# Expert weights of a mixture layer: gate and up blocks loaded in pairs, in another order

## The reference, cut to what matters

```python
probs = softmax(h @ router_w)                       # per group
gate, idx = top_k(swapaxes(probs, 1, 2), cap)       # cap = 64 latent, 16 context tokens per expert
xs = h[b_idx, idx]                                  # 80 rows of 1024 per expert
hid = silu(xs @ wg[e]) * (xs @ wu[e])               # wg, wu: 1024 x 2048 per expert
ye = (hid @ wd[e]) * gate                           # wd: 2048 x 1024 per expert
f = zeros_like(h).at[b_idx, idx].add(ye)
x = x + g2 * rms_norm(f, norm_ffn_post)
```

## Time and profile before

| | |
|---|---|
| median of 3 runs | 1744.59 us (1741.53 to 1746.22) |
| profiled execution | 1750.1 us, its span 1748.2 us |
| PE busy | 1561.2 us (89%), 7025 matmuls |
| DVE busy | 1273.4 us (73%) |
| ACT busy | 997.7 us (57%) |
| POOL busy | 199.1 us (11%) |
| weight queue (q1) | 179184 packets, 453.01 MB, 70.7% of 16 engines |
| packets under 8 KB | 172748 of 189173 |
| SP waits for DVE's `w_lo` before a load (L254) | 996.4 us in 380 waits |

### The profile page before, as it was taken

One profiled execution on the slowest core, in us unless ns is written; L12 is line 12 of the kernel. 1 busy time (PEld: TensorE's weight loads), 2 busy tenths in 40 slices (PEclk: granted clock), 3 DMA queues, 4 the chain that ended last, 5 costly groups with the idle time before them and its releaser, 6 DMA issues.

```text
span 1748.2 us, 19460 instructions
## 1 busy us (share of the span) xinstructions
PE 1561.2 (89%) x7025; PEld 1063.8 (61%) x7025; DVE 1273.4 (73%) x1133; ACT 997.7 (57%) x813; POOL 199.1 (11%) x100
## 2 busy tenths in 40 slices
PE   5799988978957999999999999998999999999992
PEld 3588766655854666666666665665665666666561
DVE  5525544774476888888888887887888878888883
ACT  6223345142334676666666676666676666766761
POOL 5411222144000000000000000000000000000000
PEclk8799999888957999999999999999999999999996
DMA  9321112347234899999999999999999999999983
GB/s 345 107 66 55 49 49 75 106 141 275 84 133 163 333 367 347 373 335 354 365 350 369 341 348 360 337 381 322 349 357 338 380 324 371 357 343 377 333 322 127
DMA packets 189173, 476.73 MB, mean 273 GB/s; under 512 B 11470, under 2 KB 13770, under 8 KB 172748
## 3 DMA queue, kind: packets, MB, share of 16 engines
q1 hardware_dynamic: 179184, 453.01, 70.7%
q0 software_dynamic: 3072, 10.49, 2.5%
q10 hardware_dynamic: 6876, 12.68, 2.1%
HBM read 462.51 MB, written 13.64 MB: 272 GB/s over the span
## 4 chain that ended last, share of the span: by engine, by line
PE 31%; DVE 22%; DMA 20%; ACT 13%; issue 12%; POOL 2%; ACTq 0%; SPq 0%; DVEq 0%; POOLq 0%
DVE w_lo L266 12%; ACT w_hi L260 11%; DMA raw<-in_exp_down 7%; DMA raw<-in_exp_gate 6%; DMA raw<-in_exp_up 4%; PE bank L298 4%; PE bank L297 4%; PE bank L299 4%; PE bank L934 3%; PE bank L938 3%; PE bank L935 3%; PE bank L919 2%; PE bank L920 2%; PE bank L924 2%; POOL w_lo L266 1%
## 5 line engine op out<-in xcount | busy, mean ns | idle before, releaser
L266 DVE TENSOR_TENSOR w_lo<-raw,w_hi 128x2048 fp32r<-128x2048 f32 (+1 forms) x424 | 946.9, 2246 | 319.8 <-ACT w_hi L260 319.5
L260 ACT CAST w_hi<-raw 128x2048 fp32r<-128x2048 f32 x424 | 805.6, 1910 | 336.6 <-PE bank L299 63.3
L919 PE MATMUL bank<-w_hi,act_lo 128*80 128x512 f32 x1024 | 407.3, 398 | 17.3 <-DVE act_lo L1358 16.7
L920 PE MATMUL bank<-w_hi,act_hi 128*80 128x512 f32 x1024 | 402.9, 393 | 0.0
L924 PE MATMUL bank<-w_lo,act_hi 128*80 128x512 f32 x1024 | 277.7, 392 | 0.7 <-DVE w_lo L266 0.7
L934 PE MATMUL bank<-w_hi,act_lo 128*80 128x512 f32 x512 | 206.4, 403 | 35.1 <-DVE act_lo L1369 34.9
L919 PEld LDWEIGHTS bank<-w_hi,act_lo 128*80 128x80 f32 x1024 | 154.3, 151 | 99.2 <-issue 16.3
L924 PEld LDWEIGHTS bank<-w_lo,act_hi 128*80 128x80 f32 x1024 | 151.3, 148 | 85.7 <-DVE w_lo L266 2.7
L935 PE MATMUL bank<-w_hi,act_hi 128*80 128x512 f32 x512 | 202.3, 395 | 0.0
L920 PEld LDWEIGHTS bank<-w_hi,act_hi 128*80 128x80 f32 x1024 | 152.2, 149 | 78.2 <-issue 0.5
L1469 POOL DMA_INDIRECT f_rows<-arena,slot_tok x16 | 26.7, 1671 | 1118.6 <-ACT arena L623 1118.6
(11 more groups left out here) (204 smaller groups left out, 1415.7 us busy)
## 6 DMA issues: line engine op xcount, KB each, us to landing
raw<-in_exp_gate SPq DMA_DIRECT2D x128, 1024.0 KB, 5.9
raw<-in_exp_up SPq DMA_DIRECT2D x128, 1024.0 KB, 6.6
raw<-in_exp_down SPq DMA_DIRECT2D x128, 1024.0 KB, 6.2
raw<-in_ada_w SPq DMA_DIRECT2D x24, 1024.0 KB, 5.5
raw<-in_w_in SPq DMA_DIRECT2D x12, 1024.0 KB, 5.0
arena<-in_x_lat ACTq DMA_DIRECT2D x8, 512.0 KB, 9.4
raw<-in_w_out SPq DMA_DIRECT2D x4, 1024.0 KB, 5.4
xn_rows<-arena SPq DMA_DIRECT2D x5, 512.0 KB, 2.6
```

Of the source, the lines that this page charges most:

```text
L260: nc.scalar.copy(w_hi[:, n % WS, :], raw[:, n % RAW, :]).then_inc(hi_done, 1)
L266: ops.tensor_tensor(w_lo[:, n % WS, at], raw[:, n % RAW, at], w_hi[:, n % WS, at], ALU.subtract).then_inc(done, 1)
L919: mm(dst, x[1][:, kk, :], wh[:, k, :], start=(kk == 0), stop=False)
L920: mm(dst, x[0][:, kk, :], wh[:, k, :], start=False, stop=False)
```

## The change

Gate and up blocks are taken in pairs: b now counts pairs of blocks (0 or 1), and a chunk of a pair is 2 k-tiles x 1024 columns, in rows of 4 KB. A pair is four chunks (`part` 0..3), and each chunk adds to two PSUM banks: gate pair in banks 0 and 1, up pair in 2 and 3. Matmuls per chunk, their shapes and the two splits stay as they were, and so do RAW and WS. The order of a body becomes g1 (4 chunks), d0, d1 (2 each), u1 (4), g0' (4), d2, d3 (2 each), u0' (4); the last body is g1 u1 d0 d1 d2 d3. Eight chunks (g0, u0) stand in front of the first body instead of six.

What hangs on the order moves with it: both silus of a pair stand at the gate pair's last chunk, both `hidden` at the up pair's last chunk and there ahead of that step's split. `turn_after` says after which chunk a block of `hid` is turned: blocks 0 and 1 after g1's parts 0 and 2, blocks 2 and 3 after g0's parts 0 and 2 (in the last body after d0 and d1). The token transposes stand after steps i = 4 and 8, `gathered` at 5 and 9. On SP the zeroing of `f_rows` comes before the writes of `xn2_rows`, both behind seven expert loads instead of six. The post-norm gain of the expert layer is loaded by SP behind the last weight load, and its products go to regions of their own.

```diff
     def body_chunks(last):
-        order = [("u", 1, 0), ("d", 0, 0), ("g", 2, 0), ("u", 2, 0), ("d", 1, 0), ("g", 3, 0), ("u", 3, 0), ("d", 2, 0)]
-        if not last:
-            order += [("g", 0, 1)]
-        order += [("d", 3, 0)]
-        if not last:
-            order += [("u", 0, 1), ("g", 1, 1)]
-        return [(kind, b, half, nxt) for kind, b, nxt in order for half in range(2)]
-
-    FIRST_CHUNKS = [(kind, b, half) for kind, b in (("g", 0), ("u", 0), ("g", 1)) for half in range(2)]
+        if last:
+            order = [("g", 1, 0), ("u", 1, 0), ("d", 0, 0), ("d", 1, 0), ("d", 2, 0), ("d", 3, 0)]
+        else:
+            order = [("g", 1, 0), ("d", 0, 0), ("d", 1, 0), ("u", 1, 0), ("g", 0, 1), ("d", 2, 0), ("d", 3, 0), ("u", 0, 1)]
+        return [(kind, b, part, nxt) for kind, b, nxt in order for part in range(2 if kind == "d" else 4)]
+
+    FIRST_CHUNKS = [(kind, 0, part) for kind in "gu" for part in range(4)]
+
+    def turn_after(last, kind, b, part):
+        at = {("g", 1, 0): 0, ("g", 1, 2): 1}
+        at.update({("d", 0, 1): 2, ("d", 1, 1): 3} if last else {("g", 0, 0): 2, ("g", 0, 2): 3})
+        return at.get((kind, b, part))
...
         w = {"g": exp_gate, "u": exp_up}[kind]
-        w = w[bass.ds(e, 1), :, b * 512:(b + 1) * 512].rearrange("o (k p) n -> p (o k) n", p=P)
-        return w[:, 4 * half:4 * half + 4, :]
+        w = w[bass.ds(e, 1), :, b * D:(b + 1) * D].rearrange("o (k p) n -> p (o k) n", p=P)
+        return w[:, 2 * part:2 * part + 2, :]
...
# sync
-        for i, (kind, b, half) in enumerate(FIRST_CHUNKS):
-            load(sync, N_EXP + i, 0, expert_source(0, kind, b, half), 512)
+        for i, (kind, b, part) in enumerate(FIRST_CHUNKS[:-1]):
+            load(sync, N_EXP + i, 0, expert_source(0, kind, b, part), D)
+        sync.wait_ge(fz, 1)
+        for t in range(TILES):
+            sync.dma_start(f_rows[t * P:(t + 1) * P, :], zeros).then_inc(f_zero, 16)
         for t in range(TILES):
             sync.wait_ge(xn2_rd, t + 1)
             sync.dma_start(xn2_rows[t * P:(t + 1) * P, :], xn2[:, t, :]).then_inc(xn2_out, 16)
...
# scalar, body
-                if not last and (kind, b, half) == ("g", 3, 0):
-                    gathered_half(e + 1, 1 - pr2, 0)
-                if not last and (kind, b, half) == ("d", 2, 0):
-                    gathered_half(e + 1, 1 - pr2, 1)
+                if not last and i in (5, 9):
+                    gathered_half(e + 1, 1 - pr2, i // 9)
                 ... split_hi(act, N_BODY + i + WS, e)
-                if half and kind == "g":
-                    silu(N_BODY + i, e, b)
-                    if b:
-                        hidT_hi(e + nxt, b - 1)
...
-                if kind == "d" and b == 2 and half:
-                    hidT_hi(e, 3)
+                if kind == "g" and part == 3:
+                    silu(N_BODY + i, e, 2 * b)
+                    silu(N_BODY + i, e, 2 * b + 1)
+                turn = turn_after(last, kind, b, part)
+                if turn is not None:
+                    hidT_hi(e, turn)
...
# tensor
-            for k in range(4):
-                kk = 4 * half + k
-                mm(dst, x[1][:, kk, :], wh[:, k, :], start=(kk == 0), stop=False)
-                mm(dst, x[0][:, kk, :], wh[:, k, :], start=False, stop=False)
+            for kk, dst, j, at in steps:
+                mm(dst, x[1][:, kk, :], wh[:, j, at], start=(kk == 0), stop=False)
+                mm(dst, x[0][:, kk, :], wh[:, j, at], start=False, stop=False)
...
# tensor, body
+                turn = turn_after(last, kind, b, part)
+                if turn is not None:
+                    if turn:
+                        pe.wait_ge(ht_lo, 4 * e + turn)
+                    hid_T(e, turn)
-                if not last and half and kind == "d" and b == 1:
+                if not last and i == 4:
                     gather(e + 1, 0)
-                if not last and half and kind == "u" and b == 3:
+                if not last and i == 8:
                     pe.wait_ge(xs_f, 2 * e + 3)
                     gather(e + 1, 1)
...
# vector, body
+                if not last and i in (5, 9):
+                    gathered(e + 1, i // 9)
+                    gathered_lo(e + 1, 1 - pr2, i // 9)
+                if kind == "u" and part == 3:
+                    hidden(N_BODY + i, e, e + nxt, 2 * b)
+                    hidden(N_BODY + i, e, e + nxt, 2 * b + 1)
                 if not last or i + WS < len(chunks):
                     split_lo(dve, "dve", N_BODY + i + WS, e)
+                turn = turn_after(last, kind, b, part)
+                if turn is not None:
+                    hidT_lo(e, turn)
```

More of the change, by code:

```diff
@@ L259, in split_hi @@
             act.wait_ge(w_used, e * PER_E + (n - WS + 1))
-        nc.scalar.copy(w_hi[:, n % WS, :], raw[:, n % RAW, :]).then_inc(hi_done, 1)
+        nc.scalar.copy(w_hi[:, n % WS, :], landed(n)).then_inc(hi_done, 1)
     def split_lo(eng, who, n, e=0):
@@ L323, in _ @@
             sync.dma_start(xn2_rows[t * P:(t + 1) * P, :], xn2[:, t, :]).then_inc(xn2_out, 16)
-        sync.wait_ge(fz, 1)
-        for t in range(TILES):
-            sync.dma_start(f_rows[t * P:(t + 1) * P, :], zeros).then_inc(f_zero, 16)
+        kind, b, part = FIRST_CHUNKS[-1]
+        load(sync, N_EXP + len(FIRST_CHUNKS) - 1, 0, expert_source(0, kind, b, part), D)
         def body(e, last):
-            for i, (kind, b, half, nxt) in enumerate(body_chunks(last)):
-                load(sync, N_BODY + i, e, expert_source(e + nxt, kind, b, half), D if kind == "d" else 512)
+            for i, (kind, b, part, nxt) in enumerate(body_chunks(last)):
+                load(sync, N_BODY + i, e, expert_source(e + nxt, kind, b, part), D)
         with sync.Fori(0, LAST) as e:
@@ L954, in _ @@
         pe.wait_ge(xs_l, 2)
-        for i, (kind, b, half) in enumerate(FIRST_CHUNKS):
-            up_or_gate(N_EXP + i, 0, b + (2 if kind == "u" else 0), half, xs[0])
-        hid_T(0, 0)
+        for i, (kind, b, part) in enumerate(FIRST_CHUNKS):
+            up_or_gate(N_EXP + i, 0, 2 if kind == "u" else 0, part, xs[0])
         def body(e, pr2, last):
-            for i, (kind, b, half, nxt) in enumerate(body_chunks(last)):
+            for i, (kind, b, part, nxt) in enumerate(body_chunks(last)):
@@ L971, in body @@
                 else:
-                    if half == 0:
+                    if part == 0:
                         pe.wait_ge(ht_lo, 4 * e + (b + 1))
-                    down(n, e, b, half)
-                if half and kind == "g" and b:
-                    if b > 1:
-                        pe.wait_ge(ht_lo, 4 * e + (b - 1))
-                    hid_T(own, b - 1)
-                if not last and half and kind == "d" and b == 1:
+                    down(n, e, b, part)
+                turn = turn_after(last, kind, b, part)
@@ L981, in body @@
+                if turn is not None:
[3 more added lines that the diff above has]
+                if not last and i == 4:
                     gather(e + 1, 0)
-                if not last and half and kind == "u" and b == 3:
+                if not last and i == 8:
                     pe.wait_ge(xs_f, 2 * e + 3)
                     gather(e + 1, 1)
-                if half and kind == "d" and b == 2:
-                    pe.wait_ge(ht_lo, 4 * e + 3)
-                    hid_T(e, 3)
-                    if last:
-                        pe.wait_ge(gbias2, 16)
-                        pe.wait_ge(sl_ev, 4 * NEXP)
-                        gate_rows(rows, (0, 1, 2, 3))
+                if last and kind == "d" and b == 2 and part == 1:
+                    pe.wait_ge(gbias2, 16)
+                    pe.wait_ge(sl_ev, 4 * NEXP)
+                    pe.wait_ge(hid_rd, 4 * NEXP)
+                    gate_rows(rows, (0, 1, 2, 3))
@@ L1248, in _, with gate_row @@
                 split_lo(dve, "dve", n)
-        def gate_row(first, banks):
+        def gate_row(first, banks, gain, dst):
             dve.wait_ge(post_in, 16 * (first // 4 + 1))
@@ L1256, in gate_row @@
                     dve.wait_ge(gr_ps, first + 2 * g + half + 1)
-                    tt(g_row[:, g, at], psum[banks[2 * g + half]][:, :], post[:, at], ALU.mult).then_inc(gr_ev, 1)
-        gate_row(0, (2, 3, 5, 6))
+                    tt(dst[g][:, at], psum[banks[2 * g + half]][:, :], gain[:, at], ALU.mult).then_inc(gr_ev, 1)
+        gate_row(0, (2, 3, 5, 6), post, [g_row[:, 0, :], g_row[:, 1, :]])
         dve.wait_ge(col_rd, 8)
```

115 lines of the change are left out of this document (52 added, 63 removed).

## The result

The changed kernel takes 1803.98 us (median of 5 runs, 1801.48 to 1813.97) against 1744.59 in the same session (1740.65 to 1748.17): ratio 1.035, interval 1.032 to 1.039. It is 59 us slower where 17 were forecast, and lies outside the range.

What follows compares the result with a forecast made beforehand. PE was taken as the bound, waiting for the in-order lists of DVE and ACT. 15 x (0.2 + 0.7) = 13.5, + 5 clock, - 1 last body = +17.5 us; 1744.6 + 17 = 1761 us, range 1734 to 1778.

Steps and rivals of the forecast that it cites:

- What bounds the kernel: In the experts PE is the bound, and it waits for the in-order lists of DVE and ACT.
- The packets: On the weight queue q1, packets were to fall by 65536, to 113.6 thousand.
- "nothing" for the moved SP and POOL steps: Later `xn2_rows` writes and gathers needed earlier were to cost nothing, having enough cover.
- Place A: Behind the gathers, to block 2's turn: PE waits 3.0 us, 2.8 before; +0.2 us per expert.
- The old waits at d2, g0' and d3 are gone: Behind the gathers: these PE waits vanish, as their data has two chunks more of time.
- Place B: Behind the scatter at time s: PE waits 1.9 us at block 1's turn, 1.17 before; +0.7 us per expert.
- The -1 for the last body: The last body loses waits at d0, d1 and d3, some 2 us, and gets one at the turn: -1 us.
- The walk to the turn of block 1: Behind the scatter at s: chunk 3's copy at s + 12.8 plus 4.8 us; PE, there at s + 15.7, waits 1.9.
- the 17 old waits that the prediction counted at d0: Behind the scatter before the change: 17 of 49 PE waits for `hidT_lo`, 1.17 us per expert with tails.
- The clock: PE's clock falls behind waits of about 2 us in 5 of 15 experts instead of 2: +5 us.
- rival 2: Much slower: the clock falls in most experts, at block 2's or block 1's turn; +33 us, 1777; chance 0.13.
- The sum: Whole kernel: 13.5 us of waiting, + 5 for the clock, - 1 for the last body, +17.5 us.

Runs made afterwards that it cites:

- E3: The changed kernel without the indirect gathers (from the second expert on) and scatters (but the last): 1746.6 us, ratio 1.003.
- E4: The kernel before the change without the indirect gathers (from the second expert on) and scatters (but the last): 1729.4 us, ratio 0.993.
- E2: The changed kernel's order, with gate and up chunks of 4 k-tiles x 512 columns in 2 KB rows: 1770.8 us, ratio 1.017.
- E13: The changed kernel with each gate and up chunk loaded by two DMAs of 512 columns, in 2 KB rows: 1804.5 us, ratio 1.035.
- E5: The changed kernel with six landed chunks instead of four in the experts: 1724.4 us, ratio 0.990.
- E6: The changed kernel's order with chunks in 2 KB rows and six landed chunks instead of four: 1724.2 us, ratio 0.989.
- E9: The changed kernel with four unused 512-column matmuls ahead of each wait at the turns of blocks 1 and 2: 1784.4 us, ratio 1.025.
- E11: The changed kernel without the scatters (but the last), gathers kept: 1751.9 us, ratio 1.004.
- E14: The changed kernel with each gate and up chunk loaded by two DMAs of one k-tile, in 4 KB rows: 1801.8 us, ratio 1.035.
- E10: The changed kernel with gate chunks of 4 k-tiles x 512 columns in 2 KB rows, up chunks in 4 KB rows: 1792.5 us, ratio 1.026.
- E15: The changed kernel with up chunks of 4 k-tiles x 512 columns in 2 KB rows, gate chunks in 4 KB rows: 1815.8 us, ratio 1.043.
- E8: The kernel before the change with six landed chunks instead of four: 1714.3 us, ratio 0.984.

## Why the prediction was wrong, step by step

**What bounds the kernel** was read rightly: PE and the in-order lists around it. The packets, the unchanged work of DVE and ACT, and "nothing" for the moved SP and POOL steps held. POOL's first gather, for one, still waits for its slot numbers and not for the later `xn2_rows`, as in the earlier trace rows:

```profile
POOL arena L1460 <- DVE slot_tok L1346: 85.0, 1, 85.0
```

**Place A** was right in size. The forecast had DVE done 25.6 us behind the transpose, 3 us of waiting, 2 of it at the turn; the trace has 25.3 and 1.65. E3 against E4 shows the waiting itself is worth nothing net (+0.2 per expert was said). Its place was right too; its consequence was not, see the clock. "The old waits at d2, g0' and d3 are gone" held.

**Place B is the first step that failed**: "Its load is still issued behind the split of chunk 23, at the same time, behind the same scatter and gather. What differs is the row length", and from that chunk 3 at s + 12.8. The issue came when it said, at s + 3.5 in both kernels, but the load took 10.6 us to land, for 9.5 before (means of 14). Chunk 3 was copied at s + 14.2, and chunk 2, of which nothing was said for the new order, at s + 10.9 instead of 8.8. E2 prices this at 33 of the 59 us. The reasoning went wrong twice. It bounded the new loads' landing by the medians of the earlier trace rows, -0.2 to +0.5 us, but those are over all loads, and what counts is the landing beside a scatter, where the trace of before had no chunk of this shape. And it took row length as the one difference; E13, with the short rows, is as slow, so row length alone is not the cause. The bound should have been as wide as the delay in hand: the scatter already held chunk 3 up by 2.7 us (13.1 for 10.4), so twice that was no remote case, and a chunk 2 that is 2 us late makes the turn of block 0 wait as well, a term that the sum did not have. The -1 for the last body lacked it too: PE waited 3.9 us there. Depth decides whether all this matters (E5 equals E6).

The walk to the turn of block 1 had the right path and a wrong start. From chunk 3's copy at s + 14.2, its 4.8 us give s + 19.0, where s + 17.6 was said. PE came to the turn at about s + 16.1, for 15.7: it ended chunk 23 near s + 6.2 and not 7.0 (s + 5.4 in the expert shown), but lost more than that at block 0. So the wait there is 2.4 us in the mean, and 0.6 at block 0, where 1.9 was said for all of place B. Of the 17 old waits that the prediction counted at d0, 9 are there (9.9 us) and 8 at d1 (3.7 us); their sum is right.

**The clock is the second**: "I take 5 falls in 15 experts instead of 2: +5 us. Bounds: 0 (-3) and 12 or more (+17)". It fell 17 times; E9 measures 19.6 us for them. 15 falls more at its own 1.7 us are 25.5, above its upper bound, and rival 2, much slower, was this with no error at place B. Most falls, 10, came at the turn of block 1 and so out of the first failure. Yet E3 shows that the waits of place A suffice for 10 falls: 1.7 us in one piece did it at a place where PE had also waited shortly before, at chunk 12. The argument against rival 2, that waits near 1 us leave the clock up, said nothing of waits near 2.

**The sum** of what the traces show: 27.5 us more of waiting and 28.4 more of busy time, some 22 of it clock, in 13 of the 15 periods; the forecast had 13.5 less 1 and 5 for all of it. That the kernel got slower was forecast, and for its two places, but the size was not. The Trainium skill's rule that all engines' DMAs interleave on the same 16 (DMA: Bandwidth & Descriptors, Issuing engines are not separate DMA queues) pointed at the right mechanism, and E11 agrees with it (52 us less without scatters). The Trainium skill's figure for the overhead of a packet (DMA: Bandwidth & Descriptors, Why small descriptors are slow), by which the long rows gain a little, is not borne out as a gain here: E6 and E5, 2 KB and 4 KB rows, differ by 0.2 us. Where the loads do set the time, E13 with 2 KB rows and E14 with 4 KB take 1804.5 and 1801.8, and their intervals overlap.

**Open.** Why chunks of 2 k-tiles x 1024 columns land later beside the scatter than chunks of 4 x 512 was not settled, nor why a mixture does not help (E10, E15). An influence of how the addresses fall on the memory is conceivable; no run tests it. Nor does one test the order of the banks alone, or a scatter that does not add.

## What to carry to other kernels

A deadline may stand behind a load only if the ring is deep enough to cover that load's slowest landing, beside whatever else uses the DMA engines at that moment, and not its median; six slots for four were worth 80 us here and 30 in the kernel before, and with them the shape of the chunks no longer mattered. Price a wait of PE of about 2 us with the clock that it may take along (it did so behind 3 to 10 of 15 such waits), and don't let several small waits become one of that size. Put a consumer one step behind the last instruction that its producer's in-order list still has in front of it: with six slots, moving three turns turned an order that lost 10 us to E8 into one that wins 11. With four slots the same edit moved the waits along.

## What was not expected of the hardware

Filling matmuls whose result nobody reads made the kernel 20 us faster (E9), by holding PE at 2.4 GHz. A megabyte in rows of the same length is copied 2 us later behind the scatter when the chunks cover half as many matrix rows, twice as wide, and come in two DMAs (E13 against E2); two DMAs for one changed nothing at 4 KB rows (E14). The DMA engines were as busy then, and moved a fifth less (268 GB/s for 339). One indirect scatter of 80 rows per expert cost the changed kernel some 3.5 us per expert (52 us over 15), where both indirect DMAs together cost the kernel before 1.0 (E4, 15 us).
